# Moving the matmul operands of a fused two-block transformer kernel to other addresses modulo 256 bytes

## What is computed

```python
def swiglu(h, w_in, w_out):
    gu = h @ w_in
    g, u = jnp.split(gu, 2, axis=-1)
    return (jax.nn.silu(g) * u) @ w_out
```

## The kernel before

| operand | bytes per tile | start modulo 256 |
|---|---|---|
| `raw`, `w_hi`, `w_lo` (a weight tile is 512 bytes) | 4096 | 128 |
| `X`, `xn` | 1024 | 128 |
| `xh`, `xl` | 1024 | 64 |
| `mean` | 512 | 192 |
| `act_hi`, `act_lo` | 1024 | 64 |
| `xr_h`, `xr_l`, tile k | 1088 = 4 x 256 + 64 | 64, 128, 192, 0, 64, 128, 192, 0 |
| `yh1`, `yl1`, `yh2`, `yl2`, `cqh`, `cql` | 1024 | 64 |

## Time and profile before

### The profile page before, as it was taken

The page is one execution under the profiler, slowest core; times in us unless marked ns, Lnnn a source line. Parts: engine busy times, 40 slices in busy tenths (PEclk is TensorE's granted clock), DMA queues, the critical chain, the costliest instruction groups (busy, mean ns, idle before and its releaser), DMA issues.

```text
span 902.7 us, 19303 instructions
## 1 busy us (share of the span) xinstructions
PE 877.4 (97%) x7318; PEld 843.5 (93%) x7318; DVE 705.1 (78%) x1100; ACT 471.2 (52%) x732; POOL 93.1 (10%) x139
## 2 busy tenths in 40 slices
PE   8999999999999999999999989899999999999996
PEld 5888898999999999999999979789998999999996
DVE  4898866989999779888887768779897888766543
ACT  4646675655554568444444455556545754444451
POOL 1032002000000320000002104000011100000000
PEclk9999999999999999999999999999999999999999
DMA  7453346566768984788889946745586467555651
GB/s 261 140 173 108 118 138 236 182 188 208 208 209 272 331 291 148 264 289 292 288 276 301 306 164 233 257 138 190 199 279 224 140 213 257 185 186 187 211 160 47
DMA packets 53335, 191.73 MB, mean 212 GB/s; under 512 B 5920, under 2 KB 6432, under 8 KB 53152
## 3 DMA queue, kind: packets, MB, share of 16 engines
q1 hardware_dynamic: 41760, 149.96, 50.5%
q0 software_dynamic: 10656, 39.33, 13.3%
q10 hardware_dynamic: 864, 1.67, 0.6%
HBM read 189.89 MB, written 1.05 MB: 212 GB/s over the span
## 4 chain that ended last, share of the span: by engine, by line
PE 89%; DVE 7%; DMA 1%; ACT 1%; issue 1%; SPq 0%; POOL 0%; DVEq 0%; ACTq 0%
PE ps L391 27%; PE ps L392 26%; PE ps L393 26%; DVE w_lo L1238 2%; DMA raw<-w 1%; PE ps L463 1%; PE ps L465 1%; PE ps L464 1%; PE ps L499 1%; DVE ada_raw L1526 1%; PE ps L556 1%; PE ps L530 1%; PE ps L470 1%; ACT w_hi L844 1%; DVE rstd_w L1243 1%
## 5 line engine op out<-in xcount | busy, mean ns | idle before, releaser
L1238 DVE TENSOR_TENSOR w_lo<-raw,w_hi 128x1024 fp32r<-128x1024 f32 x282 | 340.7, 1227 | 98.1 <-ACT w_hi L844 97.6
L391 PE MATMUL ps<-xh,w_hi 128*128 128x256 f32 x1344 | 378.3, 282 | 7.7 <-DVE w_lo L1238 4.6
L392 PE MATMUL ps<-xl,w_hi 128*128 128x256 f32 x1344 | 374.8, 279 | 0.0
L393 PE MATMUL ps<-xh,w_lo 128*128 128x256 f32 x1344 | 374.7, 279 | 0.0
L844 ACT ACTIVATE w_hi<-raw 128x1024 fp32r<-128x1024 f32 x282 | 287.9, 1052 | 45.3 <-PE ps L393 24.9
L391 PEld LDWEIGHTS ps<-xh,w_hi 128*128 128x128 f32 x1344 | 253.8, 189 | 12.6 <-issue 10.6
L393 PEld LDWEIGHTS ps<-xh,w_lo 128*128 128x128 f32 x1344 | 253.8, 189 | 0.0
L392 PEld LDWEIGHTS ps<-xl,w_hi 128*128 128x128 f32 x1344 | 252.5, 188 | 0.3 <-issue 0.2
L391 PE MATMUL ps<-act_hi,w_hi 128*128 128x256 f32 x528 | 147.8, 280 | 0.0
L393 PE MATMUL ps<-act_hi,w_lo 128*128 128x256 f32 x528 | 147.6, 279 | 0.0
L392 PE MATMUL ps<-act_lo,w_hi 128*128 128x256 f32 x528 | 147.6, 279 | 0.0
(11 more groups left out here) (262 smaller groups left out, 1138.2 us busy)
## 6 DMA issues: line engine op xcount, KB each, us to landing
raw<-w SPq DMA_DIRECT2D x282, 512.0 KB, 4.4
ada_raw<-ada_w POOLq DMA_DIRECT2D x72, 512.0 KB, 4.8
X<-x_in SPq DMA_DIRECT2D x4, 256.0 KB, 5.7
bm<-bias_in POOLq DMA_DIRECT2D x1, 1024.0 KB, 6.0
out<-X SPq DMA_DIRECT2D x4, 256.0 KB, 2.4
tab<-tab_in ACTq DMA_DIRECT2D x1, 640.0 KB, 4.5
gmask<-gmask_in ACTq DMA_DIRECT2D x1, 512.0 KB, 5.4
cact<-c_in POOLq DMA_DIRECT2D x1, 512.0 KB, 6.4
```

Of the source, the lines that this page charges most:

```text
L391: pe.matmul(o, lh, rh, start=start, stop=False, skip_group_check=True)
L392: pe.matmul(o, lh, rl, start=False, stop=False, skip_group_check=True)
L393: return pe.matmul(o, ll, rh, start=False, stop=stop, skip_group_check=True)
L1238: v.tensor_tensor(w_lo[:, slot(h), :], raw[:, slot(h), :], w_hi[:, slot(h), :].bitcast(F32), ALU.subtract).then_inc(lo_ready, 1)
```

## The change

Two of the tensors that only fill space get other sizes: `off_line` ahead of `xh` from 448 to 384 bytes per partition, `on_line` behind `xl` from 312 to 504 (320 and 512 when rounded up).

```diff
         xn = sb("xn", [P, KC, S])
-        sb("off_line", [P, 112])
+        sb("off_line", [P, 96])
         xh = sb("xh", [P, KC, S], F32R)
         xl = sb("xl", [P, KC, S], F32R)
-        sb("on_line", [P, 78])
+        sb("on_line", [P, 126])
         rstd_w = sb("rstd_w", [P, SW])
```

## The result

The changed kernel takes 916.73 us (median of 4 runs, 915.52 to 917.07), beside 907.19 us for the kernel before on the same chips (4 runs, 905.33 to 910.46). The ratio is 1.0111, 95% interval 1.0083 to 1.0139: slower by 1.1%. The forecast was 900 us. The profiled execution has a span of 913.7 us, 11.0 more than before. All instructions are the same in number and order on every engine.

What follows compares the result with a forecast made beforehand. TensorE was taken as the bound: matmul count times distance between starts. Terms of minus 5.4, minus 3.0 and plus 2.8 us gave minus 5.6 from 904.5, so 898.9; forecast 900 us, range 887 to 916.

Steps and rivals of the forecast that it cites:

- Zero for ScalarE and VectorE: Writing the `xr` tiles: ScalarE takes 492 to 498 ns; starts move both engines by 6 to 9 ns at most, no effect.
- thin VectorE cover: First feed-forward: VectorE busy 18.59 of 20 us; should TensorE speed up by 4%, VectorE at 97%, late next.
- Two distances: Split-product matmuls of 256 columns: starts 117.8 ns (long) or 113.3 ns (short) apart for the same code, constant inside a stretch.
- The price list: Settled `xr` cycle, weights at 128: per matmul 123.3 ns at start 64, 120.0 at 128, 118.3 at 192, 121.7 at 0.
- products and attention outputs, long: Their 1,202 matmuls at the long distance, moved from 64 to 192, go from 117.8 to 113.3 ns: minus 5.4 us.
- Their 630 short ones: Products and attention outputs already at 113.3 ns, 630 matmuls, stay there: no change.
- Activations, long: 1,786 activation matmuls at 117.8 ns, moved from 64 to 0, become 1.7 ns cheaper: minus 3.0 us.
- Activations, short: 992 activation matmuls at 113.3 ns, moved from 64 to 0, go to 116.1 ns: plus 2.8 us.
- The third, dearer distance: Rival: activations at 0, farthest from weights at 128, run at 120.9 ns; 918 us with products unchanged; chance 0.20.
- break-even of 119.2: With products faster by 5.4 us, slower than 913 begins where activations' mean distance exceeds 119.2 ns.
- Drawn anew: Rival: each stretch draws its distance whatever the address; 904 to 911 us, middle 908; chance 0.25.
- The rule: Independent TensorE ports and 16-byte SBUF lines make all starts at multiples of 64 alike: sum 0 instead of minus 5.6 us.

Runs made afterwards that it cites:

- the repeat: The kernel before, with no edit, measured and profiled once more on another execution: 908.99 us, span 907.1.

## Why the prediction was wrong

*What bounds the kernel.* Right: nothing but the distance between TensorE's starts changed, and the queues and other engines kept their times. Zero for ScalarE and VectorE held: ScalarE took 491 to 498 ns for an `xr_h` tile. The first feed-forward's thin VectorE cover was not called on by the change, since TensorE didn't speed up; in the run with `xr` moved it did, and VectorE was late next, as the step said: two waits for `w_lo`, 0.94 and 0.74 us.

*The reading of the rows.* Two distances and no other were rightly read; that a stretch keeps its distance isn't quite so. In the profile of before, the products behind the earlier trace rows's window of 460 to 512 us go over from 113.3 to 117.8 ns at a delay of 0.17 us over two starts, and stay there to their end:

```profile
512.21 0.28 PE L393 MATMUL ps<-act_hi,w_lo 128*128 128x256 f32 x1
512.38 0.39 PE L391 MATMUL ps<-act_hi,w_hi 128*128 128x256 f32 x1
512.61 0.28 PE L392 MATMUL ps<-act_lo,w_hi 128*128 128x256 f32 x1
```

The load of 192 ns as the mark of the long distance doesn't hold either: products at 192 run at 117.7 with loads of 187 to 188.

*The price list.* This is the step that failed: "the trace has a price list for the start modulo 256", applied to stretches that all stand on one start. The list gave 192 before 128, 0 and 64. In long uniform stretches the order is 64 (113.3 or 117.8), 192 (117.8), 0 (118.7), 128 (120.0): 64 goes from the dearest to the cheapest, and four of the six pairs stand the other way round. The weakness that the text named, "each tile there inherits the phase of its neighbour", fits that, but how six matmuls behind a tile at another start come by their price no run shows. What is shown is that the same starts have other prices, and another order, in a mixed cycle than in a stretch.

The terms, in the windows of the earlier trace rows: products and attention outputs, long, minus 5.4 us: nothing, for at 192 they stay long. Their 630 short ones "stay": they went long, plus 2.8. Activations, long, minus 3.0: plus 1.6. Activations, short, plus 2.8: plus 5.3. Minus 5.6 became plus 9.7.

*The rivals.* The third, dearer distance is what happened: one that no stretch of 256 columns had shown, at 0. Its size was off, 118.7 instead of 120.9 in the long stretches, and it would have stayed within 0.5% by its own break-even of 119.2, had the products become shorter as I then took for granted; they became longer instead. That is also why the range, which ended at 916, was missed by 0.7 us. "Drawn anew" is true of the kernel before (and of 64 bytes below), but not whatever the address: with weights at 128, no stretch at 0 or 128 had 113.3, and at 192 few had.

*The rule.* The Trainium skill gives TensorE two independent read ports (TensorE: Matmul & The Clock Gate, Part 2) and SBUF lines of 16 bytes (SBUF — State Buffer, Specifications). By both, I had concluded, all these starts are alike. The runs disagree: for one instruction stream the distance goes from 113.3 to 120.0 ns with the relative start of streamed and loaded operand, so the two do affect each other in this case. Where and how no run shows.

## What to carry over

In a stream like this one (f32r, a 128 x 128 load for every matmul of 256 columns), try other starts of the streamed operand relative to the weights modulo 256. Here the same start as the weights is the worst, 120.0 ns, and 64 bytes below them the best, 113.3 or 117.8. Read the distance from starts in long uniform stretches, never from a mixed cycle. And look at what streams just ahead of a long stretch: moving the eight tiles each of `xr_h` and `xr_l` by 64 or 128 bytes gave 0.9 to 1.1% (896.05 us, the quickest version) without moving the operands of the stretch itself.

## What I had not expected of the hardware

A stretch of some 1,340 matmuls (864 of activations and 479 of products from 360 us in the kernel before) kept one distance, 113.3 ns (117.8 in the repeat), from its first matmuls to a delay at 512.38 us, at full granted clock and with nothing to wait for, and passed it on to other tensors at the same relative start. In no profile did the mean over 30 matmuls move by more than 2 ns between one break and the next; it changed at breaks and behind other operands alone, as at the wait of 0.94 us and the delay of 0.17 us above. With the weights on the streamed operand's own place every load takes 192 ns and the distance is 120.0. What in TensorE or the memory holds such a phase no run shows.
